# A norm's sums of squares taken as columns of 128 tokens on TensorE, in a two-layer backbone step

## The reference

```python
def rms_norm(x, g):
    xf = x.astype(jnp.float32)
    y = xf * lax.rsqrt(jnp.mean(xf * xf, axis=-1, keepdims=True) + EPS)
    return (y * g.astype(jnp.float32)).astype(x.dtype)

def trunk_layer(x, c_vec, lp, ctx_cache, pos):
    shift1, scale1, gate1, shift2, scale2, gate2 = adaln(c_vec, lp['w_ada'], lp['b_ada'])
    h = rms_norm(x, lp['norm1']) * (1 + scale1) + shift1
    conv_in, q_lat, kv_lat, k_rope, gates = split_projection(h @ lp['w_in'])
...
    x = x + gate1 * ((g_conv * conv_out + g_att * att) @ lp['w_out'])
    h2 = rms_norm(x, lp['norm2']) * (1 + scale2) + shift2
    x = x + gate2 * hier_moe(h2, lp['w_group'], lp['b_group'], lp['w_expert'], lp['b_expert'],
                             lp['w1'], lp['w3'], lp['w2'])
```

## Time and profile before

| | us |
|---|---|
| median of three executions | 1003.34 |
| lowest and highest of them | 998.62, 1005.89 |
| span of the profiled execution | 1006.5 |
| layer 0: from the first square to the first use of the inverse (L1421 to L1781) | 9.39 to 22.74 |
| layer 1: the same | 515.46 to 530.43 |

### The profile page before, as it was taken

How to read it: one execution, slowest core, us unless ns; L and a number is a source line. 1 busy time by engine, 2 the same in 40 slices (tenths; PEclk the granted TensorE clock), 3 DMA queues, 4 the chain that set the end, 5 groups by cost and what they waited for, 6 DMA issues and landing times.

```text
span 1006.5 us, 15181 instructions
## 1 busy us (share of the span) xinstructions
PE 943.0 (94%) x5850; PEld 783.4 (78%) x5850; DVE 734.7 (73%) x1211; ACT 502.7 (50%) x714; POOL 63.6 (6%) x62
## 2 busy tenths in 40 slices
PE   4899999989999899999978999999999989999997
PEld 1797798867888778888857977997579977888886
DVE  4667788564855579878966587895648658997895
ACT  4343623275522367657745335324663236774772
POOL 1000000054000000000010000000820000000000
PEclk9899999999999589999998999999999978999999
DMA  9943477601555279949936435553123206994971
GB/s 375 382 145 131 172 297 275 242 1 43 223 200 205 76 264 356 369 149 350 375 124 251 168 130 205 193 231 126 43 85 126 84 12 229 353 376 161 339 286 63
DMA packets 29017, 206.71 MB, mean 205 GB/s; under 512 B 3408, under 2 KB 3440, under 8 KB 4240
## 3 DMA queue, kind: packets, MB, share of 16 engines
q1 hardware_dynamic: 28656, 204.81, 53.7%
q0 software_dynamic: 288, 0.92, 0.3%
HBM read 203.98 MB, written 1.74 MB: 204 GB/s over the span
## 4 chain that ended last, share of the span: by engine, by line
PE 81%; DVE 10%; ACT 5%; issue 2%; DMA 1%; POOL 1%; DVEq 0%; SPq 0%; ACTq 0%
PE ps L854 57%; PE ps L841 7%; PE ps L865 4%; PE ps L1255 3%; PE ps L832 2%; ACT w_hi L711 1%; PE ps L1007 1%; PE ps L1090 1%; DVE w_lo L717 1%; DVE x L2237 1%; PE ps L1078 1%; PE ps L1263 1%; DVE rs L1740 1%; ACT kT L1509 1%; DMA x<-x 1%
## 5 line engine op out<-in xcount | busy, mean ns | idle before, releaser
L722 DVE TENSOR_TENSOR w_lo<-ring,w_hi 128x2048 fp32r<-128x2048 f32 (+1 forms) x100 | 224.2, 2247 | 30.4 <-ACT w_hi L1614 30.0
L854 PE MATMUL ps<-h_hi,w_hi 128*128 128x384 f32 x576 | 198.4, 344 | 6.1 <-issue 2.4
L1614 ACT ACTIVATE w_hi<-ring 128x2048 fp32r<-128x2048 f32 x96 | 183.4, 1914 | 30.8 <-PE ps L854 30.8
L854 PE MATMUL ps<-h_hi,w_lo 128*128 128x384 f32 x576 | 193.6, 336 | 0.0
L854 PE MATMUL ps<-h_lo,w_hi 128*128 128x384 f32 x576 | 193.5, 336 | 0.0
L717 DVE TENSOR_TENSOR w_lo<-ring,w_hi 128x2048 fp32r<-128x2048 f32 x42 | 95.8, 2289 | 53.1 <-ACT w_hi L711 53.1
L854 PEld LDWEIGHTS ps<-h_hi,w_hi 128*128 128x128 f32 x576 | 108.0, 188 | 20.9 <-issue 12.8
L711 ACT ACTIVATE w_hi<-ring 128x2048 fp32r<-128x2048 f32 x44 | 83.6, 1909 | 56.9 <-DMA ring<-wpre 46.4
L854 PEld LDWEIGHTS ps<-h_lo,w_hi 128*128 128x128 f32 x576 | 108.1, 188 | 0.0
L854 PEld LDWEIGHTS ps<-h_hi,w_lo 128*128 128x128 f32 x576 | 108.0, 188 | 0.0
L1847 DVE SCALAR_TENSOR_TENSOR z<-u,par,z 128x399 f32<-128x399 f32 x180 | 104.7, 630 | 1.5
(11 more groups left out here) (266 smaller groups left out, 1466.8 us busy)
## 6 DMA issues: line engine op xcount, KB each, us to landing
ring<-wpre SPq DMA_DIRECT2D x96, 1024.0 KB, 6.5
ring<-wmoe SPq DMA_DIRECT2D x96, 1024.0 KB, 4.9
x<-x SPq DMA_DIRECT2D x1, 1536.0 KB, 7.7
x_out<-x SPq DMA_DIRECT2D x4, 384.0 KB, 2.3
par<-par_in POOLq DMA_DIRECT2D x2, 367.5 KB, 4.8
const<-const_in SPq DMA_DIRECT2D x1, 314.0 KB, 3.1
ckv_out<-ckvT POOLq DMA_DIRECT2D x2, 64.0 KB, 2.7
kr_out<-kr POOLq DMA_DIRECT2D x2, 16.0 KB, 3.4
```

The costliest lines, as they stand in the source:

```text
L722: return nc.vector.tensor_tensor(out, whole, leading.bitcast(F32), ALU.subtract)
L854: m = mm(out, a, b, start=(start and i == 0 and j == 0), stop=(stop and i == n - 1 and j == 2))
L1614: af(w_hi[m % MOE_PLACES], slot(moe_slot(l, m)), ACT.Copy).then_inc(split_hi, 1)
```

## The change

The eight squares are no longer added on VectorE. For each chunk and each of the three groups of 128 tokens, TensorE multiplies the chunk of squares, as stationary operand, by one column of ones: 24 matmuls of 128 x 1, accumulated into three columns of PSUM (token on the partition). ScalarE takes the root of 128 x 3 values, VectorE inverts 128 x 3 values, and multiplies the identity by each of the three columns, which gives three diagonal matrices side by side in `rs`. TensorE multiplies ones by these (`spread_root`, one matmul of 384 columns), which puts each token's inverse on every partition, in PSUM; the norm reads it there in place of `rs`.

Besides: in both layers the squares' matmuls come first on TensorE, ahead of the units of `w_ada`; in layer 1 one unit stands between them and spread_root, and two behind it (before: two ahead, one behind). ScalarE loads its table with the root ahead of the squares (a root of one column, thrown away), and in layer 1 also makes the hi part of lat 0 before the squares. In layer 1 VectorE makes the lo part of lat 0 in two halves of 832 columns, one before the norm and one behind its second chunk, and forms `h_lo` one chunk sooner. GpSimd waits for the eighth square, not for their sum. In layer 0 VectorE inverts and spreads the root ahead of the first gain.

```diff
@@ -267,8 +267,9 @@
             add.next = (add.next + 1) % add.banks
         jobs.append((name, index, bank, taker))
 
-    add.next, add.banks = 0, ADA_BANK
-    add("ss", 0, "act")
+    add.next, add.banks = 1, ADA_BANK
+    add("ss", 0, "act", BACK_BANKS[0])
+    add("spread", 0, "dve", BACK_BANKS[0])
     for t in range(TT):
         add("lat", t, "dve", 4 + t)
     for c in range(KC):
...
@@ -790,7 +792,7 @@
             pool.dma_start(par, par_in[0]).then_inc(par_loaded, 16)
             for l in range(LAYERS):
 
-                pool.wait_ge(squares_added, l + 1)
+                pool.wait_ge(sq_ready, l * 2 * KD + KD)
                 settle(pool)
                 nc.gpsimd.memset(u[:, :, :], 0.0).then_inc(u_cleared, 1)
 
...
@@ -941,25 +943,45 @@
 
                 def square_sum():
                     out = begin("ss", 0)
-
-                    pe.wait_ge(squares_added, l + 1)
+                    for c in range(KD):
+
+                        pe.wait_ge(sq_ready, l * 2 * KD + (c + 1))
+                        for t in range(TT):
+                            m = mm(out[:, t:t + 1], h[:, c, t * P:(t + 1) * P], ones[:, 0:1],
+                                   start=(c + t == 0), stop=(c == KD - 1 and t == TT - 1))
+                            if c + t == 0:
+                                first(m)
+                    m.then_inc(psum_full, 1)
+
+                def spread_root():
+
+                    out = begin("spread")
+                    pe.wait_ge(root_spread, l + 1)
                     mm(out[:, 0:TOK], ones, rs[:, 0:TOK], start=True, stop=True).then_inc(psum_full, 1)
 
                 def latent(c, outs):
-                    w = split_unit("lat", c // 4, 4, LAT_W)(0, LAT_W)
+                    if l > 0 and c < 2:
+
+                        pe.wait_ge(lat_begun, l)
+                    else:
+                        wait_made(pe, base, SPLIT_AT[("lat", c // 4)])
+                    n = place_of(SPLIT_AT[("lat", c // 4)])
+                    a = c % 4 * LAT_W
+                    w = [(w_hi[n][:, a:a + LAT_W], w_lo[n][:, a:a + LAT_W])]
 
                     pe.wait_ge(h_ready, l * KD + (c + 1))
                     for t in range(TT):
                         m = split_product(outs[t][:, 0:LAT_W], pairs(h_hi, h_lo, KD, t * P, (t + 1) * P)[c:c + 1],
-                                          w[c % 4:c % 4 + 1], start=(c == 0), stop=(c == KD - 1))
+                                          w, start=(c == 0), stop=(c == KD - 1))
                         if c == KD - 1:
                             m.then_inc(psum_full, 1)
                     if c % 4 == 3:
                         held.append(split_used)
 
                 if l == 0:
+                    square_sum()
                     first_rows(0, 0)
-                    square_sum()
+                    spread_root()
                     first_rows(0, 1)
                     ada_columns(1)
                     outs = [begin("lat", t) for t in range(TT)]
...
@@ -972,10 +994,11 @@
                     latent(KD - 2, outs)
                     latent(KD - 1, outs)
                 else:
-                    for e in PRE[l][:ADA_AHEAD - 1]:
+                    square_sum()
+                    ada(PRE[l][0])
+                    spread_root()
+                    for e in PRE[l][1:ADA_AHEAD]:
                         ada(e)
-                    square_sum()
-                    ada(PRE[l][ADA_AHEAD - 1])
                     outs = [begin("lat", t) for t in range(TT)]
                     for c in range(KD):
                         latent(c, outs)
...
@@ -1415,14 +1438,18 @@
                     make_hi(act, l, base, base16, n)
 
                 def norm():
+
+                    af(lat_r[:, 0:1], eps[:, 0:1], ACT.Sqrt)
+                    if l > 0:
+
+                        act.wait_ge(split_used, base)
+                        hi(0)
                     for c in range(KD):
 
                         act.wait_ge(x_moe, done * KD + (c + 1))
                         af(h[:, c, :], x[:, c, :], ACT.Square).then_inc(sq_ready, 1)
-                    if l > 0:
-                        hi(0)
                     wait_full(act, l, "ss", 0)
-                    af(rs[:, 0:TOK], ps_of("ss", 0)[:, 0:TOK], ACT.Sqrt, bias=eps[:, 0:1],
+                    af(lat_r[:, 0:TT], ps_of("ss", 0)[:, 0:TT], ACT.Sqrt, bias=eps[:, 0:1],
                        scale=1.0 / D).then_inc(taken["act"], 1)
                     hi(1 if l > 0 else 0)
                     for c in range(KD):
...
@@ -1733,20 +1760,15 @@
             for l in range(LAYERS):
                 done = rounds_before(dve, l)
                 base = splits_before(dve, l, done)
-                def add_squares(which, c):
-
-
-                    dve.wait_ge(sq_ready, l * 2 * KD + (which * KD + c + 1))
+                def add_squares(c):
+
+
+                    dve.wait_ge(sq_ready, l * 2 * KD + (KD + c + 1))
                     m = vt(rs[:, 0:TOK], h[:, 0, :] if c == 1 else rs[:, 0:TOK], h[:, c, :], ALU.add)
-                    if which == 1 and c == KD - 2:
+                    if c == KD - 2:
                         m.then_inc(sums_ready, 1)
-                    elif c < KD - 1:
+                    else:
                         chain(m)
-                    else:
-                        m.then_inc(squares_added, 1)
-
-                for c in range(1, KD):
-                    add_squares(0, c)
 
                 dve.wait_ge(par_loaded, l * 16 + 16)
 
...
@@ -1763,26 +1785,45 @@
                     gain(0, "norm1", 2 * b, 2 * b + 2).then_inc(layer_set, 1)
                     dve.wait_ge(layer_set, b + 1)
 
+                def lo(n):
+                    make_lo(dve, l, base, n)
+
+                def lat_part(a, b):
+
+                    dve.wait_ge(split_hi, base + 1)
+                    return lower(w_lo[place_of(0)][:, a:b], slot(pre_slot(l, PRE_AT[l][SPLIT[0]]))[:, a:b],
+                                 w_hi[place_of(0)][:, a:b])
+
+                def root():
+
+                    wait_taken(dve, l, "ss", 0)
+                    chain(nc.vector.reciprocal(lat_r[:, 0:TT], lat_r[:, 0:TT]))
+                    for t in range(TT):
+                        m = vs(rs[:, t * P:(t + 1) * P], ident, lat_r[:, t:t + 1], None, ALU.mult)
+                    m.then_inc(root_spread, 1)
+
                 if l == 0:
+                    root()
                     first_gain(0)
                 else:
                     dve.wait_ge(adaT_taken, batches_before(l, "ada"))
                     gain(0, "norm1").then_inc(layer_set, 1)
-
-                def lo(n):
-                    make_lo(dve, l, base, n)
+                    root()
+                    lat_part(0, 2 * LAT_W).then_inc(lat_begun, 1)
 
                 def norm(below):
 
-                    wait_taken(dve, l, "ss", 0)
-                    chain(nc.vector.reciprocal(rs[:, 0:TOK], rs[:, 0:TOK]))
+                    wait_full(dve, l, "spread")
                     for c in range(KD):
                         for st, (a, b) in enumerate(((0, CTX), (CTX, TOK))):
-                            m = stt(h[:, c, a:b], x[:, c, a:b], amp[:, 0, c, st:st + 1], rs[:, a:b], ALU.mult, ALU.mult)
+                            m = stt(h[:, c, a:b], x[:, c, a:b], amp[:, 0, c, st:st + 1], ps_of("spread")[:, a:b],
+                                    ALU.mult, ALU.mult)
                         m.then_inc(xn_ready, 1)
                         if l > 0:
-                            if c > 1:
-                                below(c - 2)
+                            if c > 0:
+                                below(c - 1)
+                            if c == 1:
+                                lat_part(2 * LAT_W, 4 * LAT_W).then_inc(split_lo, 1)
                             if c == 2:
                                 lo(1)
                         elif c % 2:
...
@@ -1805,11 +1845,12 @@
                     for st, (a, b) in enumerate(((0, CTX), (CTX, TOK))):
                         m = stt(h_lo[:, c, a:b], h[:, c, a:b], mod[:, c, st:st + 1],
                                 h_hi[:, c, a:b].bitcast(F32), ALU.add, ALU.subtract)
+                        if c == KD - 1 and st == 0:
+                            m.then_inc(taken["dve"], 1)
                     m.then_inc(h_ready, 1)
 
                 norm(below)
                 if l > 0:
-                    below(KD - 2)
                     below(KD - 1)
                 lo(2)
 
```

6 lines of the change are left out of this document (3 added, 3 removed).

## The result

| | median us | lowest to highest | executions |
|---|---|---|---|
| before | 998.67 | 996.32 to 1013.88 | 20 |
| after | 1008.79 | 1001.00 to 1016.47 | 20 |

The ratio of after to before is 1.0065, with a 95% interval of 1.0041 to 1.0089: some 6.5 us slower (4.1 to 8.9). It is not the ratio of the two medians, which lie 10.1 us apart, because it sets aside executions more than 1.5% above the fastest of their kernel (four of before at 1013.2 to 1013.9, one of after at 1016.47) and the times come in groups. The means of all twenty are 1002.5 and 1008.0, 5.4 us apart.

A forecast was written before the change was run, and what follows sets the result against it. TensorE was taken to bound the kernel, so the norm's start decides: +5.5 us in layer 0 and -2.0 in layer 1 make +3.5 on the median 1003.3, hence 1007 us, range 998 to 1012.

The forecast's parts named there:

- What bounds it: TensorE, 81% of the last chain; in both layers a shift of the norm's start shifts the layer's end about equally.
- The price of the thin matmul: The 24 matmuls of 128 x 1 cost their weight loads: 5.5 us at the high clock, 10.8 at the low.
- the last one's way through: Layer 0: 0.2 us added after the 24 thin matmuls before their sums are ready, at 20.9.
- The first rival: Weight loads don't follow the clock, 0.23 us per thin matmul: layer 0 at 0, layer 1 -3, total 1000; chance 0.10.
- Layer 0: +5.5 forecast: 24 thin matmuls at the low clock move layer 0's norm start from 22.74 to 28.3; +5.5 us taken.
- The slow rival: Layer 1 gains nothing because the clock falls before 521.5, and layer 0 adds another 1 to 2: 1011 us; chance 0.14.
- the pair of chunks at 34: Layer 0: two chunks at the low clock run into VectorE's next step, adding another 1 to 2 us.
- Layer 1: -2.0 forecast: Layer 1: norm starts 1.5 us sooner, VectorE's order gives 0.5; the clock falls 3.4 to 5.5 us after 518.7.
- the slack: Layer 1: 1.9 us before chunk 2 of `latent`, absorbing the two units behind spread_root unless the clock stays low.
- the 0.5 us of VectorE's order: Layer 1: behind the norm's start, a shorter first lo part and sooner rests gain 0.5 to 0.9 us; 0.5 taken.
- The second rival: Thin matmuls keep the clock up: it rises in layer 0 (0 us), layer 1 gains 5, total 998; chance 0.10.
- The third: Sums keep pace with ScalarE, 0.15 us or less a thin matmul: layer 0 -1.7, layer 1 -7, total 994.5; chance 0.04.

The follow-up runs named there:

- e4: Changed kernel with 12 of the 24 thin matmuls, chunks 4 to 7 left out of the sum (output differs); one execution, 999.65 us.
- e2: Changed kernel with layer 0's throwaway root, and so the table load, ahead of ScalarE's wait for `x`; one execution, 1000.91 us.
- e3: Changed kernel with 128 columns of ones instead of one as the moving side of the 24 matmuls; ratio to before 0.9994.
- e8: Changed kernel with 128 columns of ones and layer 0's table load ahead of the wait for `x`; ratio to before 1.0000.
- e9: Changed kernel with layer 0's norm as before the change and 128 columns of ones in layer 1; ratio to before 0.9953.
- e1: Changed kernel with layer 0's norm as before the change, layer 1 as changed; ratio to before 1.0023.
- after again: The changed kernel, unchanged, run once more for a second profile; one execution, 1001.29 us.
- e5: Changed kernel with two units of `w_ada` ahead of the 24 matmuls in layer 1, none between them and spread_root; one execution, 1008.48 us.
- e7: Changed kernel with fp32r ones stationary, squares moving (8 matmuls), 384-column root and inversion, no diagonals, early table load, layer 1's lo half moved; ratio to before 0.9908.
- e6: Changed kernel with squares and two columns of ones in fp32r, one record per matmul instead of two; one execution, 1000.81 us.

## Why the prediction was right, and where it was off

**What bounds it.** Right. The norm's start is carried through: from the second execution of after to e4 the norm of layer 0 moves by -6.2 us and the sigmoid by -6.4, and what lies between the sigmoids and the routing is the same in all profiles within 1.2 us. That the norm reads PSUM in place of `rs` costs nothing, as taken: four operations in 1.39 us against 1.41.

**The price of the thin matmul.** Right, and it decided. 0.22 a record and 0.44 to 0.46 a matmul at the low clock were taken from another line's weight loads; it is 0.216 and 0.432 (10.37 / 24), so 10.4 us stands for 10.8. The 0.2 us for the last one's way through, which no row had given, is 0.04 (the root starts at 21.57, the last record ends at 21.53). At the high clock 0.23 a matmul was taken; it is 0.22 (5.26 / 24). The first rival, a price that does not follow the clock, is out: 0.11 and 0.21 us a record within one stretch. With it falls, for this kernel, the Trainium skill's rule of columns over 1.2 GHz ("TensorE: Matmul & The Clock Gate", LDWEIGHTS) at the low level; at the high one its 107 ns agree with 0.11.

**Layer 0: +5.5 forecast.** The start of the norm was met, 28.45 for 28.3, by errors that cancel. The step that failed: "The first square is done at 9.39 + 0.47 = 9.86"; in after it is done at 11.02. In before the load of the root's table stands behind the squares, under VectorE's additions (12.83 to 14.11, ScalarE's timeline):

```profile
9.39 3.42 ACT L1421 ACTIVATE gates<-x 128x384 f32<-128x384 f32 x8 [4.89 <-DMA x<-x]
12.83 1.28 ACT L1425 ACT_TABLE_LOAD   x1
```

In the changed kernel the root's dummy stands ahead of the squares and behind the wait for `x`, and the load with it:

```profile
9.10 1.28 ACT L1442 ACT_TABLE_LOAD   x1 [4.74 <-DMA x<-x]
```

It put +1.4 us in the path (e2), and the first square's way to TensorE another 0.1. Against that the 24 were 0.4 cheaper than taken, the last one's way through 0.2, the gain 0.5 (the clock rose at 27.1, and L877 took 0.65 instead of 1.08), and `x` landed 0.3 sooner than in before; the two units and the spread took the 5.35 us of the working. That leaves the 0.15 between 28.45 and 28.3. Against the landing of `x` the loss is 6.0 us in both executions of after. I had weighed ScalarE's two moved steps in layer 1 alone, where they do cost nothing. The Trainium skill ("ScalarE: Activation LUTs", What ACT_TABLE_LOAD costs) gives some 1283 ns for such a load; the trace agrees with 1.28. The page adds a drain of some 1380 ns; these rows show none, since ScalarE's next operation starts at 10.39, 0.01 behind the load's end.

To this comes a second term that was not in the sum: a pair of chunks of `latent` that starts near 43.9 took 5.03 us instead of 3.47. It is there in after, e3, e8 and e9, not in the second execution of after (3.47) nor in e2: from norm to sigmoid 39.1 us with it, 37.8 without. It moves with the clock, not with the change alone. The slow rival has a term of that size ("another 1 to 2"), but for another pair, "the pair of chunks at 34". That pair cost nothing: in the second execution of after it took 6.28 us, nearly all of it at the low clock, in the first 4.97, and norm to sigmoid is 37.85 in the second, as in before.

**Layer 1: -2.0 forecast, between -3.4 and -1.0.** Measured at the sigmoid -1.1, -2.2 (e1), -3.5 (after again) and -3.5 (e2), so they fill the stated range, and the mechanism was right too: the share falls inside the 24 or right behind them. I expected the fall 3.4 to 5.5 us after the experts' sum; it came after 2.6, 3.8, 5.1 and 5.1. The fall before 521.5, from which the slow rival decides, occurred once in these (2.6 us, and the norm gained 0.5 us instead of 1.5), and then it did not push the units past the slack, since between norm and sigmoid layer 1 took 28.4 to 28.5 us in all of after, e1, e2 and e5. (In before it took 29.1: the 0.5 us of VectorE's order that I took are 0.6.)

**The second rival**, thin matmuls that keep the clock up, is out as I put it (no rise in 10.37 us). In e3, with 128 columns, the clock rose within the stretch and did not fall in layer 1. **The third**, sums that keep pace with ScalarE, needed 0.15 a matmul; it takes another form of product (e7).

**The sum.** The distances give +2.5 (after again: +6.0 and -3.5) to +6.1 (after: +7.2 with `x` brought to the same landing, -1.1), so the +3.5 of the sum lies inside what the two starts do. Two terms are shown: +0.5 at the norm of layer 0 (the table load, less what was cheaper), and up to +1.3 where the chunks of `latent` meet the low clock. The measured +6.5, between 4.1 and 8.9, is 3 us above the sum, and a good part of that is not in the starts but in which executions are compared. The profiled execution of before at 1012.79 has the long stretch behind both norms, and the four near 1013.5 that the ratio leaves out fit it. The means of all twenty are 5.4 apart; and against the mean of all 79 executions of before in the four sets on record (not all from one chip), 1003.5 us, after's 1008.0 is 4.4 above. That the forecast's 1007 us comes near the median of 1008.79 is luck in part: it stood on before's 1003.34, and before's median over twenty is 998.67.

**What stays open.** The low stretch behind the second norms is 10 to 27 us long, worth up to 8 us a layer, and lands on every kernel. Whether a kernel's own timing makes the long form more frequent is not settled. e7 came out near its distances (-9.2 for -10.1), e9 within its interval (-4.7 for -4.5 or -3.0), e8 did not (0.0 for -3.4). With the short stretch in both layers e8 would take some 993 us (an estimate: 1001.3 less the 8.3 between 193.0 and 184.7), and none of its twelve executions is below 997.3, while before and e7 reach what the same estimate gives for them (996 and 986). That speaks for timing rather than chance in e8, and no run here shows by what.

## What to carry to other kernels

A sum over partitions with the data as the stationary operand pays a weight load per 128 x 128 block and pass, with 1 column behind it as with 128; with ones as the stationary and the data as the moving operand it pays one per chunk. In layer 0 that was 10.37 us in two passes, 5.25 in one pass (e6), and 3.55 in one pass with ones stationary, where the squares set the pace (e7). Before moving work to TensorE at a place where it has been idle, price it at the low clock. And look for what else sits in an engine's queue at the moved step: the table load written behind the wait for `x` cost 1.4 us on the path, ahead of it nothing. And where the times of a kernel come in groups, look at what makes the groups before comparing medians.

## What the runs showed of the hardware that I had not expected

- Matmuls of one column and of 128 columns take the same time per record at the same clock (0.21 us at the low level, 0.11 at the high one), but the stretch of 24 takes 10.37 us with one column and 7.71 with 128 in layer 0: the clock rose inside the second and not inside the first. In layer 1 it fell inside or right behind the 24 of one column (after 2.6 to 5.1 us) and not within or behind those of 128. PE is busy for the whole window in both.
- Three operations of VectorE of 128 x 128 take 0.68 us alone, and 2.35 and 2.21 us beside a 1.85 us operation of GpSimd (e4, e6).
- The low-clock stretch behind the second norm has lengths near 10, 14, 17, 20.5 and 27.3 us over the thirteen profiles (10.2, 13.7 and 27.3 in the two of after, 17.1 and 27.3 in the two of before), and is worth up to 8 us each time. That is more than this change moved.
- The same input transfer landed at 8.97 to 9.52 us in twelve executions and at 10.52 in one, with its issue at the same 1.64.
